# A two-layer streaming encoder on eight cores: the residual stream turned so that tokens lie on partitions

## The reference

```
for layer 0: h = rmsnorm(x, a_norm);  x += GLA(h)                 # 4 heads, keys 128, values 256, chunks of 64
             h = rmsnorm(x, f_norm0); x += convFFN(h)             # layer 0's weights
for layer 1: h = rmsnorm(x, b_norm);  x += (B * conv3(C * H)) @ w_out,  B,C,H = split(h @ w_in)
             h = rmsnorm(x, f_norm1); x += convFFN(h)
return rmsnorm(x, final_norm)

convFFN(h):  g, u = split(h @ w_up);  (silu(conv3(g)) * u) @ w_down        # 2816 inner channels
GLA(h):      q,k,v,r,gl = split(h @ w_in);  per chunk c:  S = decay*S + k_dec^T v;  o = q S
             (rmsnorm_per_head(o) * gn * silu(r)) @ w_out
rmsnorm(x, g) = x * rsqrt(mean(x*x) + 1e-6) * g
```

## Time and profile before

| | |
|---|---|
| time, three runs | 1790.12 us median (1789.09 to 1811.76) |
| profiled execution | span 1788.1 us on core 1, the slowest; its own time is not recorded beside it, the median of the runs is 2.0 us above the span |
| spans of the eight cores | 1766.1 to 1788.1 us |
| PE busy | 1586.0 us, 89% of the span |
| DVE, ACT busy | 861.6 us (48%), 627.4 us (35%) |

### The profile page before, as it was taken

One profiled execution on the slowest core, in us unless ns is written; L12 is line 12 of the kernel. 1 busy time (PEld: TensorE's weight loads), 2 busy tenths in 40 slices (PEclk: granted clock), 3 DMA queues, 4 the chain that ended last, 5 costly groups with the idle time before them and its releaser, 6 DMA issues.

```text
span 1788.1 us, 20948 instructions; the slowest of 8 cores (1766.1 to 1788.1 us)
## 1 busy us (share of the span) xinstructions
PE 1586.0 (89%) x7600; PEld 757.8 (42%) x7600; DVE 861.6 (48%) x1172; ACT 627.4 (35%) x813; POOL 81.3 (5%) x123
## 2 busy tenths in 40 slices
PE   4799664996657999999999899997899999999975
PEld 4254342543433444444444344443344444444433
DVE  2210564114646553455455655555555445545554
ACT  2332443424445440441243333322344034224322
POOL 0001000010000000000000000000000000000000
PEclk9788667996778999999999999999899999999988
DMA  6453101363030211223222223230320322322013
GB/s 193 58 84 50 24 1 24 48 94 48 1 47 0 48 27 21 36 42 47 36 42 36 36 24 49 48 47 1 48 39 10 46 36 42 48 36 42 1 47 141
DMA packets 66643, 78.20 MB, mean 44 GB/s; under 512 B 4319, under 2 KB 53744, under 8 KB 66544
## 3 DMA queue, kind: packets, MB, share of 16 engines
q0 software_dynamic: 61840, 59.86, 23.0%
q1 hardware_dynamic: 4704, 17.02, 2.8%
HBM read 128.33 MB, written 8.39 MB: 76 GB/s over the span
## 4 chain that ended last, share of the span: by engine, by line
PE 82%; DVE 8%; ACT 5%; issue 3%; DMA 2%; DVEq 0%; ACTq 0%; SPq 0%
PE PS L440 34%; PE PS L476 16%; PE PS L524 9%; PE PS L710 3%; PE PS L727 3%; PE PS L834 3%; PE PS L345 3%; PE PS L565 3%; PE PS L679 2%; ACT sq_u L340 2%; PE PS L649 2%; DVE gl_tmp_u L819 2%; DVE xn_shared_u L358 1%; DVE gl_s_u L779 1%; DMA xstage_u<-x 1%
## 5 line engine op out<-in xcount | busy, mean ns | idle before, releaser
L440 PE MATMUL PS<-xn_shared_u,wring 128*128 128x512 bf16 x2816 | 609.9, 379 | 0.4 <-DVE ffn_g_u L415 0.4
L440 PEld LDWEIGHTS PS<-xn_shared_u,wring 128*128 128x128 bf16 x2816 | 275.8, 98 | 334.1 <-issue 3.0
L476 PE MATMUL PS<-ffn_h_u,wring 128*128 128x512 bf16 x1408 | 307.5, 381 | 8.8 <-DVE ostage_u L251 8.8
L476 PEld LDWEIGHTS PS<-ffn_h_u,wring 128*128 128x128 bf16 x1408 | 138.2, 98 | 176.4 <-issue 11.7
L452 ACT ACTIVATE ffn_a_u<-PS,vecs_sb 128x1024 f32<-128x1024 f32 x88 | 98.0, 1113 | 276.1 <-PE PS L440 276.1
L485 DVE TENSOR_TENSOR XT<-XT,PS 128x512 f32<-128x512 f32 x192 | 129.0, 686 | 136.3 <-PE PS L476 136.2
L458 DVE SCALAR_TENSOR_TENSOR ffn_a_u<-ffn_g_u,vecs_sb,ffn_a_u 128x1024 f32<-128x1024 f32 x88 | 113.0, 1284 | 155.0 <-ACT ffn_g_u L456 84.3
L462 ACT ACTIVATE ffn_a_u<-ffn_a_u 128x1024 f32<-128x1024 f32 x88 | 93.0, 1057 | 248.0 <-DVE ffn_a_u L460 248.0
L524 PE MATMUL PS<-xn_shared_u,wring 128*128 128x512 bf16 x768 | 167.2, 381 | 0.0
L463 DVE TENSOR_TENSOR ffn_h_u<-ffn_a_u,PS 128x1024 bf16<-128x1024 f32 x88 | 107.4, 1221 | 120.1 <-ACT ffn_a_u L462 113.2
L834 PE MATMUL PS<-gl_of_u,wring 128*128 128x256 bf16 x512 | 77.5, 319 | 47.4 <-DVE gl_of_u L822 35.0
(11 more groups left out here) (89 smaller groups left out, 1106.7 us busy)
## 6 DMA issues: line engine op xcount, KB each, us to landing
wring<-f_w_up POOLq DMA_DIRECT2D x16, 1024.0 KB, 11.8
wring<-a_w_in POOLq DMA_DIRECT2D x12, 1024.0 KB, 12.0
wring<-f_w_down POOLq DMA_DIRECT2D x44, 256.0 KB, 8.6
xstage_u<-x SPq DMA_DIRECT2D x4, 2048.0 KB, 11.7
out<-ostage_u SPq DMA_DIRECT2D x16, 512.0 KB, 2.6
wring<-f_w_up POOLq DMA_DIRECT2D x8, 768.0 KB, 10.7
wring<-b_w_in POOLq DMA_DIRECT2D x12, 512.0 KB, 8.1
wring<-a_w_out POOLq DMA_DIRECT2D x16, 256.0 KB, 6.1
```

The lines of the kernel that those rows point to most:

```text
L440: ins = nc.tensor.matmul(self.PS[:, bank0 + t, :], w.ap[:, kc, jb * 128:(jb + 1) * 128], XN[:, kc, (hh * 2 + t) * 512:(hh * 2 + t + 1) * 512],
L476: ins = nc.tensor.matmul(self.PS[:, b, :], wd[k].ap[:, m * 128:(m + 1) * 128], H[:, k, tt * 512:(tt + 1) * 512], start=(k == 0), stop=(k = ...
```

## The change

The residual becomes `X`, fp32, `[128 tokens, 16 tiles, 1024 channels]`. x is loaded into it in 16 pieces of 128 tokens, with no transpose and no barrier, and at the end each tile is normed in place and stored from it. Gains are held as rows copied to all partitions (two buffers, loaded by SP). A norm works on 128 tokens: ACT squares with a sum over the row (`accum_out`), Ln and Exp work on one column, one DVE operation makes a bf16 tile, PE turns it with eight bf16 transposes into one PSUM bank, and ACT copies it to `XN`. The down- and out-projections take 128 tokens as stationary operand and 512 columns of the weights as moving one; DVE adds into `X`. PSUM banks are handed out by age. In the up-projection the halves of the tokens are now the outer loop over the (up to) four blocks of a weight load, so the two columns that the conv carries over pass through a small buffer `HAL`. In the chunk loop one group of 128 tokens (16 matmuls, N=512) is handed out after every second chunk, in place of two groups of eight (N=256) after every chunk. The core of the diff:

```diff
+        for i in range(NTT):
+            self.sp.dma(self.X[:, i, :], xv[i], [], self.bX[i])
...
+            for i in range(NTT):
+                self.norm_tile("f_norm0", i, self.XN, self.bXN, i)
+            self.load_gamma("b_norm")
+            self.ffn(0, lambda i: self.norm_tile("b_norm", i, self.XN, self.bXN, i))
+            self.load_gamma("f_norm1")
+            self.sconv(lambda i: self.norm_tile("f_norm1", i, self.XN, self.bXN, i))
+            self.load_gamma("final_norm")
+            self.ffn(1, self.final_tile)
...
+    def rstd_tile(self, i):
...
+        s = self.nnorm % 2
+        self.nnorm += 1
+        self.act.op(self.bX[i], [self.bSQJ, self.bSS[s]], lambda: nc.scalar.activation(
+            self.SQJ[:], self.X[:, i, :], AF.Square, accum_out=self.SS[:, s:s + 1]))
+        self.act.op([self.bSS[s], self.bconst], [self.bRST[s]], lambda: nc.scalar.activation(
+            self.RST[:, s:s + 1], self.SS[:, s:s + 1], AF.Ln, bias=self.cst[:, 0:1], scale=1.0 / D))
+        self.act.op([self.bRST[s]], [self.bRST[s]], lambda: nc.scalar.activation(
+            self.RST[:, s:s + 1], self.RST[:, s:s + 1], AF.Exp, scale=-0.5))
+        return s
...
+    def norm_tile(self, gname, i, XN, bXN, t):
...
+        s = self.rstd_tile(i)
+        self.dve.op(self.bX[i] + [self.bRST[s], self.bGB[g]], [self.bXTM[s]], lambda: nc.vector.scalar_tensor_tensor(
+            self.XTM[s][:], self.X[:, i, :], self.RST[:, s:s + 1], self.GB[g][:], ALU.mult, ALU.mult))
+        b = self.bank()
+        pt = self.PS[:, b, :].bitcast(BF16).rearrange("p (k t) -> p k t", t=128)
...
+        def tr():
...
             for kc in range(KC):
+                ins = nc.tensor.transpose(pt[:, kc, :], self.XTM[s][:, kc * 128:(kc + 1) * 128], self.identb[:])
             return ins
+        self.pe.op([self.bXTM[s], self.bconst], [self.bPS[b]], tr)
+        self.copy_on(self.act, XN[:, :, t * 128:(t + 1) * 128], pt, [self.bPS[b]], [bXN[t]])
...
+    def final_tile(self, i):
...
+        s = self.rstd_tile(i)
...
+        self.dve.op(self.bX[i] + [self.bRST[s], self.bGB[g]], self.bX[i], lambda: nc.vector.scalar_tensor_tensor(
+            self.X[:, i, :], self.X[:, i, :], self.RST[:, s:s + 1], self.GB[g][:], ALU.mult, ALU.mult))
+        self.out_toks.append(self.spo.dma(ov[i], self.X[:, i, :], self.bX[i], []))
...
+    def proj_tile(self, Y, by, w, nk, i, yi):
...
+        for n in range(2):
+            b = self.bank()
...
+            def mmd():
...
+                for k in range(nk):
+                    ins = nc.tensor.matmul(self.PS[:, b, :], Y[:, k, yi * 128:(yi + 1) * 128],
+                                           w[k].ap[:, n * 512:(n + 1) * 512],
+                                           start=(k == 0), stop=(k == nk - 1))
...
+            self.pe.op(rd, [self.bPS[b]], mmd)
+            xs = self.X[:, i, n * 512:(n + 1) * 512]
+            self.dve.op([self.bPS[b], self.bX[i][n]], [self.bX[i][n]],
+                        lambda: nc.vector.tensor_tensor(xs, xs, self.PS[:, b, :], ALU.add))
...
-                    for jb in range(nb):
-                        j = j0 + jb
-                        for hh in range(2):
+                    for hh in range(2):
+                        for jb in range(nb):
+                            j = j0 + jb
...
+                            if hh == 0:
+                                self.dve.op([], [bG[s]], lambda: nc.vector.memset(Gb[s][:, 0:2], 0.0))
+                                self.act.op([bG[s]], [bHAL[jb]], lambda: nc.scalar.copy(
+                                    HAL[:, jb, :], Gb[s][:, 1024:1026]))
+                            else:
+                                self.act.op([bHAL[jb]], [bG[s]], lambda: nc.scalar.copy(
+                                    Gb[s][:, 0:2], HAL[:, jb, :]))
...
+                last = g0 == groups[-1][0]
+                for i in range(NTT):
+                    self.proj_tile(H, [bH[k][i // 8] for k in range(gn)], wd, gn, i, i)
+                    if last and i >= 1:
+                        next_tile(i - 1)
+                if last:
+                    next_tile(NTT - 1)
...
+                            for ti in range(2):
+                                def grp(ti=ti):
+                                    self.proj_tile(of, bof, wo, KC, hf * 8 + tq * 2 + ti, ti)
...
                             emit_o(c)
-                            for _ in range(2):
-                                if pending:
-                                    pending.pop(0)()
+                            if pending and c % 2 == 1:
+                                pending.pop(0)()
```

More of the change, by code:

```diff
@@ L173, with __init__ @@
 class Prog:
[L174 to L177, removed]
+    def __init__(self):
         nc = bass.Bass("TRN2", target_bir_lowering=False)
@@ L217, in sbt, with bank @@
     def sbt(self, name, shape, dtype):
-        self._uid = getattr(self, "_uid", 0) + 1
+        self._uid = self._uid + 1
         return self.nc.sbuf_tensor("%s_u%d" % (name, self._uid), shape, dtype)
[L221 to L232, removed]
+    _uid = 0
+    def bank(self, n=1):
+        best = min(self.bank_set[::n], key=lambda b: max(self.bank_age[b:b + n]))
+        for b in range(best, best + n):
+            self.bank_age[b] = self.bank_clock
+            self.bank_clock += 1
+        return best
     def vcol(self, name, j=0):
@@ L271, in build @@
             self.out_toks = []
[L272 to L297, removed]
@@ L299, in build @@
                 self.sp.wait(t)
-            for t in self.out_toks[-4:]:
+            for t in self.out_toks[-1:]:
                 self.pe.wait(t)
-    def load_x(self):
+    def rstd_tile(self, i):
         nc = self.nc
[L305 to L326, removed]
@@ L344, in mm @@
             for kc in range(KC):
-                ins = nc.tensor.matmul(self.PS[:, bank, :], self.onesD[:], SQ[s][:, kc, :],
-                                       start=(kc == 0), stop=(kc == KC - 1))
-            return ins
-        self.pe.op([bSQ[s], self.bconst], [self.bPS[bank]], mm)
-        self.rstd_from_psum(RST[s][:], self.PS[:, bank, :], [self.bPS[bank]], bRS[s])
-        return RST[s], bRS[s]
-    def norm_tile_to(self, scr, XN, bXN, gname, t, tt):
+                ins = nc.tensor.transpose(pt[:, kc, :], self.XTM[s][:, kc * 128:(kc + 1) * 128], self.identb[:])
@@ L412, in ffn @@
             A = [es.enter_context(self.sbt("ffn_a%d" % i, [128, 1024], F32)) for i in range(2)]
+            HAL = es.enter_context(self.sbt("ffn_hal", [128, 4, 2], F32))
+            bHAL = [Buf("hal") for _ in range(4)]
             bG = [Buf("g0"), Buf("g1")]
             bA = [Buf("a0"), Buf("a1")]
-            self.dve.op([], [bG[0]], lambda: nc.vector.memset(Gb[0][:, 0:2], 0.0))
             wup = self.f_w_up[l].rearrange("(kc p) c -> p kc c", p=128)
@@ L518, in sconv @@
                         s = tt % 2
-                        pb = s * 3
+                        pb = [self.bank() for _ in range(3)]
                         def mm(w, bank):
@@ L621, in gla @@
                         bE = [Buf("e0"), Buf("e1")]
-                        with ExitStack() as es2:
-                            self.rmsnorm_to(es2, XN, bXN, "a_norm", t0=hf * 2, nt=2)
+                        for i in range(8):
+                            self.norm_tile("a_norm", hf * 8 + i, XN, bXN, i)
                         self.dve.op([], [bGL], lambda: nc.vector.memset(GL[:], 0.0))
@@ L681, in mmk @@
                                 return ins
-                            self.pe.op([bXN[kc][i // 4] for kc in range(KC)] + wk.buf, [bPS[b4]], mmk)
+                            self.pe.op([bXN[i]] + wk.buf, [bPS[b4]], mmk)
                             b2 = nextbank()
@@ L753, in gla @@
                         bOT2 = [[Buf("ot") for _ in range(TQ)] for _ in range(2)]
-                        bOSQ2 = [[Buf("osq") for _ in range(TQ)] for _ in range(2)]
+                        bOSQ2 = [[Buf("osq") for _ in range(TQ)]] * 2
                         bRS = [Buf("rs") for _ in range(HEADS)]
```

275 lines of the change are left out of this document (87 added, 188 removed).

## The result

The changed kernel is slower: 1889.68 us, median of four runs (1889.18 to 2061.63), against 1791.16 us for the kernel before (1789.09 to 1811.76); ratio 1.052, interval 1.043 to 1.062. The forecast was 1870 in a range of 1835 to 1905. In some executions of either kernel, 2061.63 us among them, one die ran at a lower clock; the ratios leave these out, and where a median holds them the ratio is the figure to read. The profiled execution spans 1887.8 us on core 3; it answers to the earlier trace rows.

The account below looks back on a forecast made before the run. Long projections were taken as bound by PE streaming matmuls, with other time at the seams, which the change rewrites. Seams: -12 + 21 + 49 + 34 + 22 - 50 + 16 = +80; 1790 + 80 = 1870 us, range 1835 to 1905.

Parts of the forecast that it names:

- The sum: Whole kernel: the changes at all seams add up to +80 us, from 1790 to 1870 us.
- One norm tile, added up: A norm tile of 128 tokens with nothing beside it is one serial chain of 5.5 us, bounds 4.9 and 6.0.
- Load and first norm: Start of the kernel: first tile lands near 9.6 us, eight tiles end at 52.5 against 64.4, minus 12 us.
- Before feed-forward 0: Norm ahead of feed-forward 0: 16 tiles, 87 us against 40.2, plus 47, and plus 2 for PE's cold start.
- Down-projection with norms: Last down-projection of feed-forward 0: PE stands 2.36 us a tile, 96 us against 63.7, with cold start plus 34.
- the conv mixer: Its out-projection: the same kind of stall, 6.3 us a tile, 105 us against 82.9, plus 22.
- cold down-projections: Rival, chance 0.06: PE falls to 1.2 GHz in the tile-wise stages, +110 us, 1980 us in all.
- GLA state loop: Chunk loop: the tile emitted behind the next chunk's output adds 2.6 us in each of six periods, plus 16 us.
- Early clock: First half's projections: slowest core's clock of 0.82 costs about 20 us; range (-20, 0); part of a 1815 us rival, chance 0.08.
- The end: From the last up-projection on: final tiles put nothing on PE, 55.6 us against 106, minus 50 us.
- At nothing: Items put at no cost: swapped operands, the gains' loads, `HAL`'s 88 copies and the zero fill on DVE.
- The faster rival: Rival, chance 0.06: the norm is pipelined at ACT's own 2.7 us a tile, and the kernel takes 1716 us.

Follow-up runs that it names:

- the norms emitted ahead: Changed kernel, but in the three norms with nothing beside them a tile's transposes and copy follow the next tile's statistics: 1816.03 us, ratio 1.0245.
- the transposes a tile later: Changed kernel, but in the two projections with norms beside them transposes and copy come one tile later, behind the next tile's matmuls: 1797.03 us, ratio 1.0137.
- the filled stall: Changed kernel with seven more matmuls a tile, results never read, ahead of the transposes in the two projections with norms beside them: 1869.6 us.
- Half groups: Changed kernel, but the chunk loop's output projection is handed out in one-bank groups of 8 matmuls after every chunk: 1869.12 us.
- The three edits: Changed kernel with norms emitted ahead, transposes a tile later and half groups together: median 1722.67 us, ratio 0.9593 to the kernel before.

## Why the prediction was right, point by point

**The sum.** 98.5 us measured, 80 forecast, every seam with its sign. Three sizes were off, and one came in that the sum had left out. That the total comes so near is in part luck: by the table the costs came out 37 us above the forecast, and 17.3 us of slow clock, which the kernel before had in this comparison and the sum did not count, gave back nearly half of it. Against the kernel before as it ran later, the kernel with the loop order undone is some 115 us slower (ratio 1.065).

**One norm tile, added up.** 5.58 us against 5.5. Square 1.06 and the accumulator read 0.19, Exp 0.2, scaling 1.28, transposes 1.03 and copy 1.01 were priced right; Ln took 0.30 in place of 0.2. That ACT's order makes the chain serial was shown by the norms emitted ahead: 2.8 us a tile, 74 us.

**Load and first norm**, -7.0 in place of -12: the first tile landed at 12.7 us and not at 9.6, and ACT loaded a table (1.28 us) before its first Square.

**Before feed-forward 0**, +58.6 in place of +49. The step that failed is the start that I read as the kernel before's. The earlier trace rows show the chain, and the chain begins at 559.54 with feed-forward 0's second unit. The timeline of PE of the kernel before shows the first:

```profile
552.11 7.07 PE L440 MATMUL PS<-xn_shared_u,wring 128*128 128x512 bf16 x32
559.54 2.75 PE L440 MATMUL PS<-xn_shared_u,wring 128*128 128x512 bf16 x12 [0.36 <-DVE ffn_g_u L415]
```

PE had done 32 matmuls between the last sums and the last scalings, since these waited only for the first 1024 tokens. So 7 us of the old norm had been covered, and the new one covers nothing. The 90 us from the last addition to the first unit were near the forecast's 87.

**Down-projection with norms**, +48.5 in place of +34, and the conv mixer +25.8 in place of +22. The stall was right (2.14 us of idling against 2.36) and so was its cause, which the transposes a tile later removed. The mis-sized term is the clock: I let it stay high, because one gap of 3.27 us in the kernel before had left it high. The same timeline has a second gap, which the prediction does not weigh:

```profile
1250.92 12.21 PE L565 MATMUL PS<-sc_y_u,wring 128*128 128x512 bf16 x48 [4.36 <-DVE XT L574]
```

After 4.36 us of idling the same 48 matmuls took 12.21 us (granted clock 0.86), so in that stage the clock did fall. With a gap of 2.14 us in each 5.8 us, nine tiles of 14 cost 1.7 us more, 15 us in all, and four in the conv mixer 6.7 us. The rival "cold down-projections" had the mechanism and priced it as all or nothing, 110 us; the filled stall showed it at 20.

**GLA state loop**, +16.8 against +16. Half groups took 20.5 us off. The edit changed both parts of the step, the additions that stood ahead of the next states and the start behind the next chunk's output. The timelines put the growth at the second: 3.1 us more ahead of the first tile and 0.4 less behind it in the period shown. No run changed one of them alone.

**Early clock.** 17.3 us of the kernel before's time, in its first projections, were a granted clock of 0.82; the changed kernel has none of it (1.00). In the kernel before only cores 0 and 1 had it, and the other six spanned 1766 to 1772 us; in the later comparisons the kernel before is 12 to 17 us faster than in the first. The prediction had it in the range and in a rival, not in the sum. Why it was there is left open; no run was made to find it.

**The end**, -50.3 against -50. **At nothing:** the loop order (1.3 us), `HAL` and the swapped operands cost what was said. In both kernels 448 matmuls of an up-projection take 96.69 us and 224 of a down-projection 48.35; feed-forward 1's middle is 1.4 us longer, all of it in its first up-projection, which now starts cold (112.86 us against 111.46).

**The faster rival** asked for a tile of 3.0 us. The three edits reach 2.8 us and no stall, and give 0.959 of the kernel before; the mechanism named there is what was shown, and the changed kernel as written does not have it.

## What to carry to other kernels

When a step is cut into finer pieces, write down for each engine the order in which it is told to work, and ask what stands behind each wait: here a copy that waited for two engines stood ahead of the next piece's start, and a set of transposes stood right behind the matmuls whose additions it had to wait for. Moving both by one piece turned a kernel 5 to 6% slower than the old one into one 4% faster (with the output projection of the chunk loop handed out in halves), with no work taken away. And read the start of a stage from the engine's timeline, not from the chain of waits, which leaves out work that was done in a gap.

## What the runs showed of the hardware

A PE that idles 2.14 us in every 5.8 us has its clock fall to 1.2 GHz in 9 of 14 tiles (granted 0.84 over the stage), while a single gap of 3.27 us had left it high and one of 4.36 us had not (0.86); with the same 2.14 us in every 6.2 it fell in 4 of 14 (0.91); 1.5 us of useless matmuls in each gap of both stages brought 0.98 in the first and 20 us in all. A Square with a sum over its row is two instructions on ACT, 1.06 and 0.19 us. With sixteen loads of 512 KB of x queued on SP, a weight load issued at 8.9 us landed 37 us later; the median of loads of that kind in that kernel is 14.7 us.
